# One step of a hybrid encoder: the sample's value tile in fp32 products side by side, w_o's adds on GpSimd, a key load and a memory key rearranged

## The chip, the cores and the metric

The kernel is one program on one core of a Trainium2 chip. The metric is device time in microseconds of that core: the median of three runs of the kernel before is 816.82 us (816.26 to 816.88). Engines are named as in the profile: PE (TensorE), DVE (VectorE), ACT (ScalarE), POOL (GpSimd) and SP (the queue that issues most DMAs).

## The reference, cut to what matters

One layer over 512 prompt and 64 sample tokens (576 in all, width 1024), in float32:

```python
h = rms_norm(x, g_mix)
z = h @ w_in                       # q_f, k_f, v_f, f_logit, c_q, c_kv, k_r
ckv = rms_norm(c_kv, g_ckv)        # returned, and expanded to keys and values
fox_o = attend(q_f, k_f, v_f, ...) # 8 heads x 64, forgetting gate, causal
mla_o = attend(mla_q, mk, mv, ...) # 8 heads, low-rank
mixed = concat([rms_norm(fox_o, g_fox_out), rms_norm(mla_o, g_mla_out)])
x = x + mixed @ w_o
m = rms_norm(mem, g_mem_src); mem_k, mem_v = m @ w_mk, m @ w_mv
x = x + attend(rms_norm(x, g_mem) @ w_mq, mem_k, mem_v) @ w_mo
hf = rms_norm(x, g_ffn)
x = x + (silu(hf @ w_gate) * (hf @ w_up)) @ w_down
return rms_norm(x, g_final), fox_k, fox_v, logf, ckv, kr, mem_k, mem_v
```

The change touches `v_f` (returned as fox_v) for the 64 sample tokens, the way of `ckv` to memory, the product with `w_o` for its fox half, and `mem_k`.

## The kernel before

**Numbers in two parts.** Nearly every weight product is made of three matmuls (`product`, L495 to L501): operand a is held as a high part in fp32r (`hhi`, `whi`) and a rest (`hlo`, `wlo`), and PE adds high x high, high x low and low x high. ACT makes the high parts (`split(b)`, the copy of L1121), POOL or DVE the rests (`rest(b)` at L2243, `weight_rest` at L1758). Some products are made in plain fp32 instead; each of those is two records of MATMUL in the trace (two passes over the moving operand), while a transposition and an fp32r product are one. `columns` (L517) sums squares over partitions with plain fp32 products by a column of ones; `spread` (L525) and `turn` (L658) are transpositions.

**Weights.** The layer's weights before the feed-forward part come in 49 blocks of the tensor `w_front`. SP's `load(b)` (L2410) brings block b into `wraw[:, b % 2]` as soon as the rest of block b-2 is made (`f_lo`), ACT's split fills `whi[:, b % 3]`, POOL's or DVE's rest `wlo[:, b % 3]`. So wraw is double and the parts are triple buffered. PE takes block b after `f_lo` has reached b+1.

**The value stage.** Blocks 7 to 10 are the value weights, 256 rows each (two k steps of 128). For each of the eight k, PE makes five token tiles: tokens stand still in the array (128, for the last tile 64), and 512 weight columns move. Sums lie in banks 0 to 4. After blocks 7, 8 and 9 come small fp32 groups (sums of squares, or spreads of their roots), which DVE and ACT turn into norms. DVE then scales the five tiles into `vst` (L1711), ACT copies them to `va`, SP sends them out. Next PE takes blocks 11, 12 and 13 (query and key weights) and goes over to attention.

**The key latents.** `ckvf` is scaled by DVE in two pieces (L1706, semaphore `s_kvn`). ACT makes `ckvhi` of each. SP sends the pieces out as `out_ckv` (L2455, `s_kvst`), and POOL, which makes the rests `ckvlo` (L2267), waits for `s_kvst` first. POOL's order is rest(11), ckvlo 0, rest(12), ckvlo 1, rest(13).

**Attention.** One loop over steps s from 0 to 95 is written out for each engine: at step s PE makes the scores of tile s (s below 80), a piece of other work (`filler`, at steps given by tables such as `WO_AT` and `RB_AT`), and the transposition of tile s-2. Other engines have the same loop and evict at step s what PE made at s-1. The filler at `WO_AT` is the product with the fox half of w_o, half a tile (128x288) each, 16 in all; DVE multiplies each by rstd into `evt` (L1847) and adds that to `xa` (L1849). The one at `RB_AT` spreads the reciprocal sums of a pair of heads; the last is at steps 86 and 87. PE leaves a spot in its banks 6 and 7 to be used again once DVE has evicted it (`spot_free`). The pieces `values(p)` (L676) and `sample_values(p)` (L692) multiply two heads at once: plain fp32, a stationary operand of 64 columns each, the results in the two halves of the partitions. `memory_keys(m)` makes a head of the memory's keys, eight k steps of three products.

Of the kernel before, what the change touches and what calls it, by code (L numbers as in the profile page):

```python
# [10 lines left out]
ALU = mybir.AluOpType  # L11
# [96 lines left out]
def build(nc, i_, o_, cum_dram):  # L108
# [93 lines left out]
    bias, _ = place("bias", [8, 3, NK], F32R, rbase + 2 * rsize)  # L202
    qt, _ = place("qt", [128, T], F32, sqbase)
# [43 lines left out]
    with ExitStack() as ctx:  # L247
# [78 lines left out]
        s_y, s_yst, d_half, s_xg = sem("s_y"), sem("s_yst"), sem("d_half"), sem("s_xg")  # L326
# [167 lines left out]
        def _(pe):  # L494
# [70 lines left out]
            columns(0, sqacc).then_inc(n_col, 1)  # L565
# [9 lines left out]

            pe.wait_ge(n_rs, 1)
# [4 lines left out]
            for c in range(4):  # L581
                b = B_V + c
                pe.wait_ge(f_lo, b + 1)
                for kk in range(2):
                    k = 2 * c + kk
                    for tt in range(TT):
                        a, n = 128 * tt, tok(tt)
                        mm = product(ps[0:n, tt, :], [t[:, k, a:a + n] for t in x1],
                                     [front(b, lo, 2, 512)[:, kk, :] for lo in (0, 1)], k == 0, k == 7)
                    if k == 0:  # L590
                        pe.wait_ge(s_cqacc, 2)
                        columns(5, sq2)
# [189 lines left out]
            def memory_keys(m):  # L782

                b = B_MK[m]
                pe.wait_ge(f_lo, b + 1)
                for k in range(KT):
                    mm = product(ps[:, m, 0:NM], [front(b, lo, KT, 128)[:, k, :] for lo in (0, 1)],
                                 [t[:, k, :] for t in (memh, meml)], k == 0, k == KT - 1)
                mm.then_inc(f_used[b % 3], 1)

            for s in range(LAST):
# [298 lines left out]
            for half in range(2):  # L1090
# [18 lines left out]
                if half == 0:  # L1109
                    mm.then_inc(d_half, 1)  # L1110
# [6 lines left out]
        def _(act):  # L1117
# [70 lines left out]
            act.wait_ge(s_init, 2)  # L1188
# [398 lines left out]
        def _(dve):  # L1587
# [31 lines left out]
            add_square(7)  # L1619
            dve.wait_ge(s_hlo, KT)  # L1620
            v.memset(vst[64:128, 6, :], 0.0).then_inc(s_init, 1)
# [87 lines left out]
            for tt in range(TT):  # L1709
                n = tok(tt)  # L1710
                v.tensor_scalar(vst[0:n, tt, :], ps[0:n, tt, :], small[0:n, S_RCM + tt:S_RCM + tt + 1], None, ALU.mult)\  # L1711
                    .then_inc(s_vev, 1)
# [76 lines left out]
            def evicted(s):  # L1789
# [431 lines left out]
            dve.wait_ge(d_half, 1)  # L2221
# [11 lines left out]
        def _(pool):  # L2233
# [69 lines left out]
            for s in range(LAST + 1):  # L2303
# [30 lines left out]
                if s - 1 in HIGH_AT and s not in (HIGH_AT[0] + 1, HIGH_AT[4] + 1):  # L2334
# [3 lines left out]
                    g.tensor_tensor(sqacc[:, 0:T], sqacc[:, 0:T], tmp2[:, j % 2, :], ALU.add).then_inc(s_oacc, 1)  # L2338

# [65 lines left out]
        def _(sp):  # L2405
            def load(b):

                need(sp, f_lo, b - 1)
                n = BLOCK_COLS[b]
# [24 lines left out]
            sp.wait_ge(s_init, 2)  # L2434
# [14 lines left out]
            load(12)  # L2449
            sp.dma_start(maskf[:, :], i_["consts"][:, C_MASK:C_MASK + 576]).then_inc(s_mask, 16)  # L2450
            sp.dma_start(maskm[:, :], i_["consts"][:, C_MASK + 576:C_END]).then_inc(s_mask, 16)
            sp.wait_ge(s_lf, 1)
            sp.dma_start(o_["logf"], lfk[:, 0:T]).then_inc(s_out, 16)
            sp.wait_ge(s_kvn, 2)
            sp.dma_start(o_["ckv"].rearrange("p (k n) -> p k n", k=2), ckvf[:, :, 0:T]).then_inc(s_kvst, 16)  # L2455
# [279 lines left out]
```

## Time and profile before

| | us |
|---|---|
| median of three runs | 816.82 |
| the profiled execution | 816.31 |
| its span in the trace | 814.4 |
| PE busy | 798.5 (98%) |
| DVE busy | 549.1 (67%) |
| ACT busy | 408.8 (50%) |
| POOL busy | 331.8 (41%) |

The profiled execution's time holds 1.9 us outside the span, and is 0.51 us under the median. Busy time of PE is the union of its instructions, which overlap: each record lasts some 0.15 us longer than the distance to the next start. So what an instruction costs on a full PE is the distance between starts, not its duration. The profile's granted clock of PE is at full speed (9 in tenths) in all but the last of the 40 slices.

### The profile page before, as it was taken

Reading aid. Unit: us, or ns where it says so; the run is one execution under the profiler, and the core shown is the slowest. Engines: PE = TensorE matmul, PEld = TensorE weight load, DVE = VectorE, ACT = ScalarE, POOL = GpSimd, SP = SyncE. Lnnn points to the kernel's source line nnn. Section 1 sums busy time; section 2 is a strip of 40 time slices with the busy share of each in tenths; the row PEclk is TensorE's granted clock in tenths of the full one; section 3 lists DMA queues with packets and bytes.
Section 4 is the critical chain, followed back from the end, with each engine's and each line's share of the span. In section 5 each row is a group of like instructions: output and inputs, shape, how many; then the busy total and the mean of one; then the engine's idle time right before and its main releaser. Section 6 shows DMA issues by size and latency. Waiting matters only on the chain.

```text
span 814.4 us, 15952 instructions
## 1 busy us (share of the span) xinstructions
PE 798.5 (98%) x5842; PEld 761.2 (93%) x5842; DVE 549.1 (67%) x986; ACT 408.8 (50%) x753; POOL 331.8 (41%) x242
## 2 busy tenths in 40 slices
PE   7999999999999999999999999999999999999996
PEld 7987998888988999998999999999999999999996
DVE  6355467887779748467599989998889985212213
ACT  7462475666777325555474555455554464322221
POOL 3664963383112126640654333333323336543420
PEclk9999999999999999999999999999999999999998
DMA  8333432110025234330133322223322332323103
GB/s 262 104 115 114 159 94 68 36 47 27 27 102 198 78 105 129 105 111 20 52 104 105 105 97 64 96 103 103 103 82 74 101 117 76 113 74 95 46 2 116
DMA packets 26518, 75.90 MB, mean 93 GB/s; under 512 B 2896, under 2 KB 7448, under 8 KB 26328
## 3 DMA queue, kind: packets, MB, share of 16 engines
q1 hardware_dynamic: 26176, 74.87, 28.7%
q8 instruction: 36, 0.59, 0.3%
q10 hardware_dynamic: 288, 0.30, 0.1%
q14 instruction: 18, 0.15, 0.1%
HBM read 68.62 MB, written 6.53 MB: 92 GB/s over the span
## 4 chain that ended last, share of the span: by engine, by line
PE 92%; DVE 3%; issue 2%; ACT 1%; DMA 0%; POOL 0%; DVEq 0%; ACTq 0%
PE ps L499 28%; PE ps L500 27%; PE ps L501 27%; PE ps L658 2%; PE ps L676 2%; PE ps L926 1%; PE ps L517 1%; PE ps L525 1%; DVE xb L2217 1%; PE ps L641 1%; PE ps L911 1%; PE ps L640 1%; DVE probs L1770 0%; ACT probs L1121 0%; DMA wraw<-w_front 0%
## 5 line engine op out<-in xcount | busy, mean ns | idle before, releaser
L499 PE MATMUL ps<-hhi,whi 128*128 128x288 f32 (+1 forms) x896 | 267.6, 299 | 6.1 <-DVE hlo L1609 5.7
L500 PE MATMUL ps<-hhi,wlo 128*128 128x288 f32 (+1 forms) x896 | 265.8, 297 | 0.0
L501 PE MATMUL ps<-hlo,whi 128*128 128x288 f32 x800 | 237.3, 297 | 0.0
L1121 ACT ACTIVATE whi<-wraw 128x1024 fp32r<-128x1024 f32 (+3 forms) x138 | 114.8, 838 | 135.6 <-PE ps L501 122.7
L499 PEld LDWEIGHTS ps<-hhi,whi 128*128 128x128 f32 x896 | 169.6, 189 | 7.7 <-DVE hlo L1609 5.7
L500 PEld LDWEIGHTS ps<-hhi,wlo 128*128 128x128 f32 x896 | 169.4, 189 | 0.2
L501 PEld LDWEIGHTS ps<-hlo,whi 128*128 128x128 f32 x800 | 151.1, 189 | 0.0
L2386 POOL TENSOR_TENSOR wlo<-wraw,whi 128x512 fp32r<-128x512 f32 x60 | 78.5, 1322 | 146.9 <-ACT whi L1121 146.9
L2243 POOL TENSOR_TENSOR wlo<-wraw,whi 128x256 fp32r<-128x256 f32 (+2 forms) x83 | 89.5, 1104 | 97.8 <-ACT whi L1121 97.6
L501 PE MATMUL ps<-hidlo,whi 128*128 128x288 f32 (+2 forms) x352 | 104.2, 296 | 0.0
L2400 POOL TENSOR_TENSOR wlo<-wraw,whi 128x1024 fp32r<-128x1024 f32 (+1 forms) x24 | 59.3, 2477 | 72.9 <-ACT whi L1121 72.9
L501 PE MATMUL ps<-tl,whi 128*128 128x288 f32 x240 | 71.5, 298 | 0.0
L500 PE MATMUL ps<-th,wlo 128*128 128x288 f32 x240 | 71.4, 298 | 0.0
L499 PE MATMUL ps<-th,whi 128*128 128x288 f32 x240 | 71.0, 296 | 0.0
L1121 ACT ACTIVATE whi<-ss 128x512 fp32r<-128x512 f32 x61 | 38.3, 631 | 63.7 <-PE ps L501 36.5
L501 PEld LDWEIGHTS ps<-hidlo,whi 128*128 128x128 f32 x352 | 66.3, 188 | 0.0
L2188 DVE TENSOR_TENSOR tmp<-ps,rstd 128x576 f32<-128x576 f32 (+2 forms) x9 | 6.2, 690 | 87.1 <-PE ps L501 87.1
L500 PE MATMUL ps<-hidhi,wlo 128*128 128x288 f32 (+2 forms) x192 | 57.0, 297 | 0.0
L499 PE MATMUL ps<-hidhi,whi 128*128 128x288 f32 (+2 forms) x192 | 57.0, 297 | 0.0
L1121 ACT ACTIVATE probs<-probs,small 128x128 f32<-128x128 f32 (+4 forms) x72 | 40.1, 557 | 32.8 <-DVE small L1770 32.4
L499 PEld LDWEIGHTS ps<-th,whi 128*128 128x128 f32 x240 | 45.3, 189 | 0.0
L500 PEld LDWEIGHTS ps<-th,wlo 128*128 128x128 f32 x240 | 45.2, 188 | 0.0
(292 smaller groups left out, 1799.4 us busy)
## 6 DMA issues: line engine op xcount, KB each, us to landing
wraw<-w_ff SPq DMA_DIRECT2D x44, 512.0 KB, 4.1
wraw<-w_front SPq DMA_DIRECT2D x41, 512.0 KB, 3.7
wraw<-w_down SPq DMA_DIRECT2D x16, 512.0 KB, 3.6
wraw<-w_down SPq DMA_DIRECT2D x8, 384.0 KB, 3.2
wraw<-w_front SPq DMA_DIRECT2D x7, 384.0 KB, 3.6
xa<-x_t SPq DMA_DIRECT2D x8, 288.0 KB, 4.8
xs<-x_t SPq DMA_DIRECT2D x7, 288.0 KB, 5.6
out_fox_k<-kt SPq DMA_DIRECT2D x4, 288.0 KB, 2.5
```

Source lines behind the costliest of these rows:

```text
L499: nc.tensor.matmul(out, lh, rh, start=start, stop=False)
L500: nc.tensor.matmul(out, ll, rh, start=False, stop=False)
L501: return nc.tensor.matmul(out, lh, rl, start=False, stop=stop)
L517: mm = nc.tensor.matmul(ps[:, bank, at + tt:at + tt + 1], source[:, 128 * tt:128 * tt + 128], ones[:, 0:1], start=True, stop=True)
L525: mm = nc.tensor.transpose(out[:, at:at + n], col[0:n, tt:tt + 1].to_broadcast([n, 128]), ident[0:n, 0:n])
L640: nc.tensor.matmul(out, q1[r][:, q], k1[r][:, ks], start=True, stop=False)
L658: mm = nc.tensor.transpose(ps[:, 2 + s % 2, 128 * kb:128 * kb + 128], probs[:, P_AT[u] + 128 * kb:P_AT[u] + 128 * kb + 128], ident[:, :])
L676: mm = nc.tensor.matmul(ps[64 * e:64 * e + 64, 4, 128 * kb:512], va[:, g, kb, h + e, :], pt[e][:, 512 * kb:512 * kb + 512 - 128 * kb], sta ...
L1121: return nc.scalar.activation(out, src, func, **kw)
L2243: mm = g.tensor_tensor(wlo[:, b % 3, c], wraw[:, b % 2, c], f(whi[:, b % 3, c]), ALU.subtract)
L2386: g.tensor_tensor(w_operand(1, j), src, f(w_operand(0, j)), ALU.subtract).then_inc(g_lo, 1)
L2400: g.tensor_tensor(ffw(n, 1, 1, w)[:, 0, :], (wraw2, wraw)[n % 4 // 2][:, n % 2, 0:w], f(ffw(n, 0, 1, w)[:, 0, :]), ALU.subtract).then_inc( ...
```

## The change

Four edits, and some semaphores that follow from them.

1. **The sample's value tile.** DVE makes one new tile `hs`, the 64 sample tokens times the gain in plain fp32, and PE multiplies it with the unsplit weights in `wraw`: per k step two products, columns 0 to 255 into partitions 0 to 63 of bank 4 and columns 256 to 511 into partitions 64 to 127, each with 64 stationary and 256 moving columns. The three products of 64 x 512 per k step go. The new products stand at the head of each of the four blocks (`sample_part`). Since PE now reads `wraw`, the loads of blocks 9 to 12 wait for it too (`p_part`), and the mask loads are issued ahead of block 12's. The fifth column of the first sums of squares is made twice, for both halves of the partitions, and DVE scales the tile in two pieces of 64x256.
2. **w_o's adds.** The 16 adds of `evt` to `xa` go from DVE to POOL, a step's turn after DVE's multiply. DVE waits for the add before last before it writes the same half of `evt` again.
3. **The key latents' way out** is issued from ACT's queue, between its two copies, and no longer from SP's.
4. **Memory key 0** is made in two parts: k steps 0 to 5 at step 85, where all eight were, and 6 and 7 at step 87, behind the last RB transpositions.

```diff
@@ build
+    hs, c2 = place("hs", [128, KT, TS], F32, rbase + rsize - 2 * NK * 4)
@@ tensor
-            columns(0, sqacc).then_inc(n_col, 1)
+            columns(0, sqacc, 4)
+            for e in range(2):
+                mm = nc.tensor.matmul(ps[64 * e:64 * e + 64, 0, 4:5], sqacc[:, TP:T], ones[:, 0:1], start=True, stop=True)
+            mm.then_inc(n_col, 1)
...
+            def sample_part(b):
+
+                for k in (2 * (b - B_V), 2 * (b - B_V) + 1):
+                    for e in range(2):
+                        at = 512 * (k % 2) + 256 * e
+                        mm = nc.tensor.matmul(ps[64 * e:64 * e + 64, 4, 0:256], hs[:, k, :], wraw[:, b % 2, at:at + 256],
+                                              start=k == 0, stop=k == 7)
+                mm.then_inc(p_part, 1)
+
+            pe.wait_ge(s_init, 2)
...
                 pe.wait_ge(f_lo, b + 1)
+                sample_part(b)
                 for kk in range(2):
                     k = 2 * c + kk
-                    for tt in range(TT):
-                        a, n = 128 * tt, tok(tt)
-                        mm = product(ps[0:n, tt, :], [t[:, k, a:a + n] for t in x1],
+                    for tt in range(4):
+                        a = 128 * tt
+                        mm = product(ps[:, tt, :], [t[:, k, a:a + 128] for t in x1],
...
                 if s == 85:
-                    memory_keys(0)
+                    memory_keys(0, 0, 6)
                 elif s == 87:
+                    memory_keys(0, 6, KT)
@@ scalar
-            for j in range(2):
-                act.wait_ge(s_kvn, j + 1)
-                activation(ckvhi[:, j, :], ckvf[:, j, :]).then_inc(s_kvhi, 1)
+            act.wait_ge(s_kvn, 1)
+            activation(ckvhi[:, 0, :], ckvf[:, 0, :]).then_inc(s_kvhi, 1)
+            act.wait_ge(s_kvn, 2)
+            nc.scalar.dma_start(o_["ckv"].rearrange("p (k n) -> p k n", k=2), ckvf[:, :, 0:T]).then_inc(s_kvst, 16)
+            activation(ckvhi[:, 1, :], ckvf[:, 1, :]).then_inc(s_kvhi, 1)
@@ vector
+            v.tensor_tensor(hs[:, :, :], xs[:, :, TP:T], gains[:, G_MIX:G_MIX + KT].unsqueeze(2).to_broadcast([128, KT, TS]), ALU.mult)\
+                .then_inc(s_init, 1)
...
-                        if s == at:
-                            dve.wait_ge(s_x[m], 32)
-                            if m == 0:
-                                dve.wait_ge(s_fev, nth(FR_AT + 1) + 1)
+                        if s == at and m == 0:
+                            dve.wait_ge(s_fev, nth(FR_AT + 1) + 1)
+                        need(dve, s_xa1, 2 * m + half - 1)
                         v.tensor_tensor(evt[:, c], spot(n, HT), rstd[:, c], ALU.mult).then_inc(s_fev, 1)
-                        dve.wait_ge(s_fev, n + 1)
-                        v.tensor_tensor(xa[:, m, c], xa[:, m, c], evt[:, c], ALU.add).then_inc(s_xa1, 1)
@@ gpsimd
+                for m, at in enumerate(WO_AT):
+                    if s - 1 in (at, at + 1):
+                        half = s - 1 - at
+                        c = slice(half * HT, half * HT + HT)
+                        if half == 0:
+                            pool.wait_ge(s_x[m], 32)
+                        pool.wait_ge(s_fev, nth(s - 1) + 1)
+                        g.tensor_tensor(xa[:, m, c], xa[:, m, c], evt[:, c], ALU.add).then_inc(s_xa1, 1)
@@ sync
                 need(sp, f_lo, b - 1)
+                if B_V + 2 <= b < B_V + 6:
+                    sp.wait_ge(p_part, b - B_V - 1)
...
```

What this makes of the order of instructions is shown at three places. The first is PE between the value stage's first and second block. `sqacc` is the sum of squares of the latents, `hhi` and `hlo` the tokens, `whi` and `wlo` the weights; a row names the moving operand's and the stationary operand's tiles. Before:

```order
L501 MATMUL ps<-wlo,hhi 128x512
L499 MATMUL ps<-whi,hhi 64x512
L500 MATMUL ps<-whi,hlo 64x512
L501 MATMUL ps<-wlo,hhi 64x512
L517 MATMUL ps<-ones,sqacc 128x1 [waits s_kvacc]
L517 MATMUL ps<-ones,sqacc 128x1 x4
L499 MATMUL ps<-whi,hhi 128x512 [waits f_lo]
L500 MATMUL ps<-whi,hlo 128x512
```

and after the change:

```order
L503 MATMUL ps<-wlo,hhi 128x512
L519 MATMUL ps<-ones,sqacc 128x1 [waits s_kvacc]
L519 MATMUL ps<-ones,sqacc 128x1 x4
L586 MATMUL ps<-wraw,hs 64x256 [waits f_lo]
L586 MATMUL ps<-wraw,hs 64x256 x3
L501 MATMUL ps<-whi,hhi 128x512
L502 MATMUL ps<-whi,hlo 128x512
```

The three products with 64 tokens that end each k step are gone, and four plain fp32 products with `hs` stand once per block, behind the small fp32 group.

The second place is DVE at steps 78 to 80 of the attention loop, where `pt` is the copy of transposed scores that PE's next transposition and values wait for. Before:

```order
L1847 TENSOR_TENSOR evt<-ps,rstd 128x288 [waits s_fdone]
L1849 TENSOR_TENSOR xa<-xa,evt 128x288 [waits s_fev]
L1888 SCALAR_TENSOR_TENSOR hlo<-olof,gains,hhi 128x576 [waits s_osq,s_ohi]
L1773 TENSOR_REDUCE small<-ps 64x1 [waits s_ex,s_qk]
L1847 TENSOR_TENSOR evt<-ps,rstd 128x288 [waits x_tile1,s_fdone]
L1849 TENSOR_TENSOR xa<-xa,evt 128x288 [waits s_fev]
L1783 COPY pt_73<-ps 128x3x128 [waits s_pvp,s_tr]
L1847 TENSOR_TENSOR evt<-ps,rstd 128x288 [waits s_fdone]
L1849 TENSOR_TENSOR xa<-xa,evt 128x288 [waits s_fev]
L1877 RECIPROCAL small<-small 128x10 [waits s_rb,s_ex]
```

and after:

```order
L1871 TENSOR_TENSOR evt<-ps,rstd 128x288 [waits s_fdone]
L1910 SCALAR_TENSOR_TENSOR hlo<-olof,gains,hhi 128x576 [waits s_osq,s_ohi]
L1798 TENSOR_REDUCE small<-ps 64x1 [waits s_ex,s_qk]
L1871 TENSOR_TENSOR evt<-ps,rstd 128x288 [waits s_xa1,s_fdone]
L1808 COPY pt_73<-ps 128x3x128 [waits s_pvp,s_tr]
L1871 TENSOR_TENSOR evt<-ps,rstd 128x288 [waits s_xa1,s_fdone]
L1899 RECIPROCAL small<-small 128x10 [waits s_rb,s_ex]
```

The adds to `xa` are gone from between the copy of `pt` and what stood ahead of it; the multiplies into `evt` now wait for POOL's adds (`s_xa1`).

The third place is SP's queue from the output of the rotary key on. Before, with blocks 11 and 12 in one row (x2) and `out_ckv` in the queue:

```order
L2447 DMA out_kr<-krf 32x576 [waits s_kr]
L2410 DMA wraw<-w_front 128x1024 [waits f_lo] x2
L2450 DMA maskf<-consts 128x576
L2451 DMA maskm<-consts 128x512
L2453 DMA out_logf<-lfk 8x576 [waits s_lf]
L2455 DMA out_ckv<-ckvf 256x1x576 [waits s_kvn]
L2410 DMA wraw<-w_front 128x1024 [waits f_lo]
```

and after:

```order
L2479 DMA out_kr<-krf 32x576 [waits s_kr]
L2442 DMA wraw<-w_front 128x1024 [waits p_part,f_lo]
L2481 DMA maskf<-consts 128x576
L2482 DMA maskm<-consts 128x512
L2442 DMA wraw<-w_front 128x1024 [waits p_part,f_lo]
L2485 DMA out_logf<-lfk 8x576 [waits s_lf]
L2442 DMA wraw<-w_front 128x1024 [waits f_lo]
```

Block 12's load has moved behind the two mask loads and waits for PE (`p_part`), and `out_ckv` is no longer in this queue.

## Rows read from the trace of the kernel before

**Rows 1.** The page: span, and part 1 (engine, busy us, share, instructions).

```profile
span 814.4 us, 15952 instructions
PE 798.5 (98%) x5842; PEld 761.2 (93%) x5842; DVE 549.1 (67%) x986; ACT 408.8 (50%) x753; POOL 331.8 (41%) x242
```

**Rows 2.** Busy time by stretch: the value stage (us and count of each engine).

```profile
47.87:79.74 31.87, 31.87 (x152) 24.60 (x151) 13.98 (x19) 14.40 (x17) 16.01 (x17) 1.00 0.41 128
```

**Rows 3.** Timeline of PE, value stage: start us, us, engine line op out<-in xcount.

```profile
50.68 0.39 PE L499 MATMUL ps<-whi,hhi 128*64 128x512 f32 x1
...
51.37 1.17 PE L517 MATMUL ps<-ones,sq 128*128 128x1 f32 x10
52.40 0.48 PE L499 MATMUL ps<-whi,hhi 128*128 128x512 f32 x1
52.72 0.40 PE L500 MATMUL ps<-whi,hlo 128*128 128x512 f32 x1
```

**Rows 4.** Timeline of PE: first pair of heads, two 64-column halves side by side.

```profile
123.44 2.37 PE L676 MATMUL ps<-pt,va 128*64 128x512 f32 x16
125.74 0.40 PE L499 MATMUL ps<-hhi,whi 128*128 128x288 f32 x1
...
128.11 0.57 PE L692 MATMUL ps<-pt,va 128*64 128x64 f32 x12
128.61 0.44 PE L658 MATMUL ps<-ident,probs 128*128 128x128 f32 x2
```

**Rows 5.** Timeline of PE: the sample's values of the last pair of heads.

```profile
265.00 0.29 PE L501 MATMUL ps<-hlo,whi 128*128 128x288 f32 x1
265.22 0.57 PE L692 MATMUL ps<-pt,va 128*64 128x64 f32 x12
265.72 0.40 PE L499 MATMUL ps<-hhi,whi 128*128 128x288 f32 x1
```

**Rows 6.** Timeline of PE, steps 81 and 82 (L658 is the transposition of step 79).

```profile
259.84 0.27 PE L761 MATMUL ps<-ident,rb 128*128 128x128 f32 x1
260.62 0.52 PE L658 MATMUL ps<-ident,probs 128*128 128x128 f32 x3 [0.51 <-DVE pt L1783]
261.12 0.65 PE L676 MATMUL ps<-pt,va 128*64 128x512 f32 x2
```

**Rows 7.** Timeline of DVE just before that.

```profile
256.68 1.34 DVE L1849 TENSOR_TENSOR xa<-xa,evt 128x288 f32<-128x288 f32 x1
...
259.54 0.46 DVE L1849 TENSOR_TENSOR xa<-xa,evt 128x288 f32<-128x288 f32 x1
259.92 0.55 DVE L1783 COPY pt<-ps 128x384 f32<-128x384 f32 x1
```

**Rows 8.** Timeline of POOL at the same place.

```profile
256.28 1.42 POOL L2338 TENSOR_TENSOR sqacc<-sqacc,tmp 128x576 f32<-128x576 f32 x1 [6.11 <-ACT tmp L1121]
```

**Rows 9.** Timeline of PE after memory key 0, and two products of key 1.

```profile
274.11 0.51 PE L517 MATMUL ps<-ones,msq 128*128 128x1 f32 x4
274.94 0.40 PE L499 MATMUL ps<-hhi,whi 128*128 128x288 f32 x1 [0.33 <-DVE olof L1832]
...
281.66 0.28 PE L499 MATMUL ps<-memh,whi 128*128 128x256 f32 x1
281.78 0.28 PE L500 MATMUL ps<-memh,wlo 128*128 128x256 f32 x1
```

**Rows 10.** Timeline of SP's queue: block 12's load, the latents' way out.

```profile
63.30 0.33 SPq L2410 DMA_DIRECT2D wraw<-w_front  x1
...
74.32 0.65 SPq L2455 DMA_DIRECT2D out_ckv<-ckvf  x1
```

**Rows 11.** Timeline of POOL: low parts of the latents and of block 12.

```profile
78.20 1.98 POOL L2267 TENSOR_TENSOR ckvlo<-ckvf,ckvhi 128x832 fp32r<-128x832 f32 x1 [7.96 <-DMA out_ckv<-ckvf]
80.14 2.84 POOL L2243 TENSOR_TENSOR wlo<-wraw,whi 128x256 fp32r<-128x256 f32 x4
```

**Rows 12.** Timeline of PE: the first product with block 12.

```profile
86.14 0.30 PE L499 MATMUL ps<-hhi,whi 128*128 128x288 f32 x1
```

More of the change, by code:

```diff
@@ L202, in build @@
     bias, _ = place("bias", [8, 3, NK], F32R, rbase + 2 * rsize)
+    hs, c2 = place("hs", [128, KT, TS], F32, rbase + rsize - 2 * NK * 4)
+    assert c2 <= rbase + rsize - NK * 4
     qt, _ = place("qt", [128, T], F32, sqbase)
@@ L325, in build @@
         w_vec, w_copy, t_f, x_hf, s_dsc = sem("w_vec"), sem("w_copy"), sem("t_f"), sem("x_hf"), sem("s_dsc")
-        s_y, s_yst, d_half, s_xg = sem("s_y"), sem("s_yst"), sem("d_half"), sem("s_xg")
+        s_y, s_yst, p_part, s_xg = sem("s_y"), sem("s_yst"), sem("p_part"), sem("s_xg")
         past = slice(T, NK)
@@ L780, in filler, with memory_keys @@
                 mm.then_inc(s_fdone, 1)
-            def memory_keys(m):
+            def memory_keys(m, k0=0, k1=KT):
                 b = B_MK[m]
                 pe.wait_ge(f_lo, b + 1)
-                for k in range(KT):
+                for k in range(k0, k1):
                     mm = product(ps[:, m, 0:NM], [front(b, lo, KT, 128)[:, k, :] for lo in (0, 1)],
                                  [t[:, k, :] for t in (memh, meml)], k == 0, k == KT - 1)
-                mm.then_inc(f_used[b % 3], 1)
+                if k1 == KT:
+                    mm.then_inc(f_used[b % 3], 1)
             for s in range(LAST):
@@ L1109, in _ @@
                 if half == 0:
-                    mm.then_inc(d_half, 1)
+                    mm.then_inc(p_part, 1)
             pe.wait_ge(r_sq, 16 + KT + 1)
@@ L1187, in _ @@
             act.wait_ge(s_cv, 48)
-            act.wait_ge(s_init, 2)
+            act.wait_ge(s_init, 3)
             for t in (5, 6):
@@ L1619, in _ @@
             add_square(7)
+            v.tensor_tensor(hs[:, :, :], xs[:, :, TP:T], gains[:, G_MIX:G_MIX + KT].unsqueeze(2).to_broadcast([128, KT, TS]), ALU.mult)\
+                .then_inc(s_init, 1)
             dve.wait_ge(s_hlo, KT)
+            dve.wait_ge(s_init, 2)
             v.memset(vst[64:128, 6, :], 0.0).then_inc(s_init, 1)
@@ L1708, in _ @@
             used(dve, B_V + 3)
[L1709 to L1712, printed above, removed]
+            for tt in range(4):
+                v.tensor_scalar(vst[:, tt, :], ps[:, tt, :], small[:, S_RCM + tt:S_RCM + tt + 1], None, ALU.mult).then_inc(s_vev, 1)
+            for e in range(2):
+                a = slice(64 * e, 64 * e + 64)
+                mm = v.tensor_scalar(vst[0:64, 4, 256 * e:256 * e + 256], ps[a, 4, 0:256], small[a, S_RCM + 4:S_RCM + 5], None, ALU.mult)
+            mm.then_inc(s_vev, 1)
             def query_dup(c):
@@ L2220, in _ @@
             low, high = slice(0, LAST_AT[1]), slice(LAST_AT[1], T)
-            dve.wait_ge(d_half, 1)
+            dve.wait_ge(p_part, 5)
             residual(KT - 1, KT - 1, low, ps[:, 6, 0:low.stop], lambda a: a)
@@ L2433, in _ @@
                 load(b)
-            sp.wait_ge(s_init, 2)
+            sp.wait_ge(s_init, 3)
             sp.wait_ge(s_sq, KT)
@@ L2448, in _ @@
             load(11)
-            load(12)
             sp.dma_start(maskf[:, :], i_["consts"][:, C_MASK:C_MASK + 576]).then_inc(s_mask, 16)
             sp.dma_start(maskm[:, :], i_["consts"][:, C_MASK + 576:C_END]).then_inc(s_mask, 16)
+            load(12)
             sp.wait_ge(s_lf, 1)
             sp.dma_start(o_["logf"], lfk[:, 0:T]).then_inc(s_out, 16)
-            sp.wait_ge(s_kvn, 2)
-            sp.dma_start(o_["ckv"].rearrange("p (k n) -> p k n", k=2), ckvf[:, :, 0:T]).then_inc(s_kvst, 16)
             load(13)
```

## The prediction, on record before the changed kernel ran

> **What bounds the kernel now.** I read the page first: PE is busy 798.5 us of a span of 814.4 [rows 1]. A full PE can still be waiting inside that number, since records overlap, so I went on to the stretch that the largest edit touches: in the value stage, 47.87 to 79.74, PE is busy all 31.87 us at a clock of 1.00 [rows 2]. There and nearly everywhere the distance between the starts of two matmuls is what counts: work taken off PE comes off the time, work added adds to it, and the other engines matter only where PE waits for them. The timeline has few such waits; two lie at places that the change touches: before the transposition at 260.62 and before the product at 274.94 [rows 6, 9].
>
> **Part 1, the value tile: what goes.** One k step's three products of 64 tokens by 512 columns run from 50.68 to 51.37 [rows 3]: 0.695 us (0.69 in the rows' rounding), 0.232 each, no less than with 128 tokens. There are eight k steps: 8 x 0.695 = 5.56 us go.
>
> **What comes.** 16 plain fp32 products, 64 stationary and 256 moving columns, in pairs for the two halves of the partitions. The trace has this form: `values` multiplies two heads side by side. Its 16 records (4 pairs of 512, 384, 256 and 128 columns, 2 passes each) take 123.44 to 125.74 = 2.30 us, which I count as 2 x 1280 = 2560 columns of pairs; `sample_values` has 6 passes of 64 = 384 columns in 128.11 to 128.61 = 0.50 us [rows 4]. The difference, 1.80 us for 2176 columns, is 0.212 us per pass of a pair of 256. Whether the two members truly run together, or in turn at a pace like fp32r's (5120 columns at 0.232 per 512 would be 2.32 us), these rows can't tell; the new products have the same form, so the price is the same. The new work is 8 pairs x 2 passes x 0.212 = 3.39 us.
>
> A visit to the half-width form costs something by itself. From [rows 4]: 0.50 - 1.5 x 0.212 = 0.18 us between first start and the next instruction's. Before it, 265.00 to 265.22 is 0.22 where 288 columns take 0.13 (256 take 0.12 [rows 9]): 0.09 more [rows 5]. Behind it, the first fp32r product takes about 0.1 longer, as behind the sums of squares (52.40 to 52.72 is 0.32 against 0.23 [rows 3]). So a visit from fp32r and back is 0.18 + 0.09 + 0.10 = 0.37. Block 7 pays that. Blocks 8 to 10 are entered from a small fp32 group whose way back is paid already: I take 0.27 for the one behind the sums of squares, and 0.18 for the two behind spreads, which end in another array form. Sum 1.00 us.
>
> What the row shows first: 0.09 us in and 0.18 around each visit. The Trainium skill (TensorEngine Tiling, Tiling Modes, Key Properties) says that changing the tiling mode, as opposed to the tile, drains TensorE. Our trace agrees. A reader who counted only the columns would have -2.17 us for this part; with the drains it is little over half of that.
>
> The first sums of squares: five full columns take 1.03 us [rows 3], 0.21 each. Now four, and two of half width: about 0.40 (0.18 + 0.09 + 2 x 0.053, and a little for the way out) for 0.21, +0.19 us.
>
> Part 1 on PE: -5.56 + 3.39 + 1.00 + 0.19 = **-0.98 us**. Bounds: -2.0 if all entries but one are free, -0.4 if every visit costs 0.37 and more.
>
> DVE's new multiply for `hs` falls into the first half of the start-up phase, ahead of a memset; the memset and SP's loads of old values wait for it, some 0.6 us, long before use. Evicting the tile in two pieces adds some 0.2 us on DVE, beside 12 us of products with blocks 11 and 12. I take nothing for either; without cover they'd cost what they last.
>
> **The held loads.** Four loads now wait for PE's new products, and block 12's moves from 63.30 [rows 10] to after the head of the fourth block, some 47.87 + 3 x 7.8 + 1.1 = about 72.5. ACT's split and the other chains on ACT slip by 2 to 3 us at block 9. Block 12 is the tightest: POOL does ckvlo 0 first, which waits for `out_ckv`, issued at 74.32 and landed at 78.20 [rows 10, 11], 3.9 us. Moved to ACT's queue it starts about 0.5 us earlier in absolute time, and so do its inputs; but block 12, block 13 and the latents are now under way together. With a landing at 78.5: ckvlo 0 till 80.5, block 12's rest (2.84 us [rows 11]) till 83.4. PE wants it at 86.14 - 1.0 = 85.1 [rows 12]. Slack 1.7 us, so nothing.
>
> **Part 2, the adds.** The wait before the transposition at 260.62: start to start 0.78 from 259.84, where such a transposition takes 0.11, and the group itself 0.50 to 261.12 for some 0.35: 0.67 + 0.15 = 0.82 us [rows 6]. The row names DVE's copy of `pt`, which began at 259.92, the moment the add from 259.54 was through [rows 7]; ahead of it DVE was late already through the add at 256.68, which took 1.34 us. Without the adds the copy starts at least 0.38 us earlier, probably over 0.6. But the values at 261.12 also wait for ACT's copy of the tile before, which hangs on the same DVE chain through an exponential, and follows it only in part. I take **-0.45 us**, bounds 0 and -0.82. What would be late next is that copy of ACT's. POOL is mostly idle there; an add is half of its 576-wide one, 1.42 / 2 = 0.7 us [rows 8], and the final multiply-add of xa comes microseconds later.
>
> **Part 3, key 0 in two parts.** The product at 274.94 waited for DVE to evict the spread of a pair of heads: 0.83 us for the four records from 274.11, where ten take 1.03 [rows 3, 9], so 0.42 of stall. Six products of 256 columns (6 x 0.12 = 0.7 us) now stand inside it and cover it wholly; they had to be made anyway. Their own change from transposition to fp32r and back costs some 0.15. **-0.27 us**, bounds +0.15 and -0.42. Block 27 comes free 0.5 us later for ACT's split of 30, whose user is 5 us off.
>
> **Sum.** -0.98 - 0.45 - 0.27 = -1.70 us. Profiled execution: 816.31 - 1.70 = 814.61, which is 0.51 under the median shown; against the median of 816.82 that is **815.1 us**. Own range of this case 814.2 to 816.0. All later stages are PE's in the same way, so what is won by 300 stays won.
>
> **Rivals.**
> *The port.* [rows 7, 8]: DVE's add of 256.68, two operands in SBUF, lasted 1.34 us where the others last 0.46, and ended 0.3 us after POOL's 256.28 + 1.42 = 257.70: it stood behind POOL's instruction. By this kernel's trace, then, 16 new POOL adds of 0.7 us can each hold a DVE instruction of that kind (`hlo`, `meml`, `wlo`), which costs more than the 0.46 that DVE saves: 3 adds before the hand-off x 0.25 = 0.75 later rather than earlier. Sum: -0.98 - 0.27 + 0.75 = -0.5, 816.3. Against it: the DVE instruction right behind the multiply starts before the semaphore reaches POOL, and then POOL stands behind it. The skill (GPSIMD Engine Reference, Specifications) states the sharing for just such instructions, those with two SBUF inputs; the trace agrees. Chance 0.17.
> *The late block*, slower than before. If the three transfers land together late, 6 us after issue, near 80, and POOL's rest takes 4 us instead of 2.84 because DVE is at work, block 12 is ready at 80 + 2 + 4 = 86 and more, and block 14's load, which waits for it in SP's queue, holds back the rests of the first keys: PE waits at 85 and again at the first scores. It decides from a landing of 80.3 us on; with 3.5 us of waits in all the sum is +1.8, 818.6; with 1.5 us it is no change. For it: queueing of a kind that no transfer there had before. Chance 0.08.
> *Not side by side.* In `values` each half has its own operands. If two halves with the same stationary tile and one block of moving weights take twice as long, that is 3.39 more: +1.7, 818.5. Against it: in [rows 4] too the form is all that the array sees. Chance 0.03.
> *More.* Both waits gone and entries cheap: -2.0 - 0.8 - 0.4 = -3.2, 813.6. Chance 0.05.
> The forecast has the rest, 0.67.
>
> **How the numbers follow.** 0.2% is 1.6 us, about what can be told from no change, and my sum sits at that line. Of the forecast's 0.67 I count 0.44 as faster and 0.23 as same; "more" is faster; the port is same but for 0.02; the late block is half slower, half same; the third is slower. Faster 0.51, same 0.42, slower 0.07. Range 813.6 to 817.0: the port's 816.3 and the mild late block are in it, the strong ones out.
>
> **What would show it.** L586 (the new products): 32 records at starts 0.21 apart in pairs, four groups, 0.3 to 0.4 us of extra at each; the value stage 1.1 to 1.2 us shorter (the columns' 0.19 lie ahead of it). No idle time of PE between 80 and 99. The transposition near 259 waits under 0.3 us. No wait at the product behind `msq`'s columns. DVE's two-input instructions in 254 to 262: if several last over 1 us, the port rival is at work. I am wrong if the value stage is not shorter by at least 0.5 us, or if PE idles before its first product with block 12, 13 or the first scores.

## The result and the profile after

| | median us | runs |
|---|---|---|
| before | 816.77 (815.94 to 817.55) | 17 |
| changed | 818.3 (816.83 to 818.89) | 17 |

The ratio is 1.0016, with a 95% interval of 1.0009 to 1.0022: the changed kernel is slower by 0.7 to 1.8 us. Forecast were 815.1, and 817.0 as the upper end. The profiled execution of the changed kernel took 816.83, the lowest of its 17; by how much and why is told below.

The page of the changed kernel (span and part 1, as in [rows 1]):

```profile
span 814.8 us, 15994 instructions
PE 797.5 (98%) x5852; PEld 759.7 (93%) x5852; DVE 544.3 (67%) x972; ACT 409.0 (50%) x753; POOL 346.8 (43%) x258
```

PE has 1.0 us less to do and the span is 0.4 longer: work was taken away and waits came in. Busy time by stretch finds them. The first row is the value stage, which answers to [rows 2]; the second goes from its end to the first scores (us, then busy us and count of PE, PEld, DVE, ACT, POOL, then granted clock, DMA share, GB/s):

```profile
47.74:78.30 30.56, 30.56 (x159) 23.47 (x159) 12.12 (x19) 14.74 (x17) 11.99 (x16) 1.00 0.40 121
78.30:100.10 21.80, 19.64 (x145) 19.22 (x144) 10.72 (x13) 10.35 (x13) 18.12 (x18) 1.00 0.44 149
```

The value stage is full, and 1.3 us shorter than 31.87. The next stretch has the same 145 records as before, but PE is idle for 2.16 us of it. Before, the same stretch lasted 19.20 us and was full. PE's timeline of the changed kernel at the two places:

```profile
84.61 0.30 PE L503 MATMUL ps<-hlo,whi 128*128 128x288 f32 x1
86.46 0.37 PE L501 MATMUL ps<-hhi,whi 128*128 128x288 f32 x1 [1.55 <-POOL wlo L2265]
...
99.19 0.29 PE L503 MATMUL ps<-hlo,whi 128*128 128x288 f32 x1
100.10 0.30 PE L656 MATMUL ps<-k,q 128*128 128x128 f32 x1 [0.62 <-issue]
```

86.46 is the first product with block 12 [rows 12]. From the start before it 1.85 us pass where 0.13 are normal: 1.7 us lost. 100.10 is the first product of scores; 0.91 after the start before it, so another 0.8 lost. "issue" hides a wait for several semaphores; GpSimd's timeline names it. Here is POOL, and ahead of it ACT's queue and SP's queue of the same kernel:

```profile
73.26 0.67 ACTq L1220 DMA_DIRECT2D out_ckv<-ckvf  x1
```

```profile
65.30 0.33 SPq L2442 DMA_DIRECT2D wraw<-w_front  x1
...
72.75 0.33 SPq L2442 DMA_DIRECT2D wraw<-w_front  x1
73.12 0.33 SPq L2485 DMA_DIRECT2D out_logf<-lfk  x1
73.50 0.33 SPq L2442 DMA_DIRECT2D wraw<-w_front  x1
```

```profile
81.59 1.98 POOL L2289 TENSOR_TENSOR ckvlo<-ckvf,ckvhi 128x832 fp32r<-128x832 f32 x1 [8.59 <-DMA out_ckv<-ckvf]
83.53 2.78 POOL L2265 TENSOR_TENSOR wlo<-wraw,whi 128x256 fp32r<-128x256 f32 x4
86.27 2.19 POOL L2289 TENSOR_TENSOR ckvlo<-ckvf,ckvhi 128x832 fp32r<-128x832 f32 x1
88.42 3.05 POOL L2265 TENSOR_TENSOR wlo<-wraw,whi 128x256 fp32r<-128x256 f32 x4
91.55 2.92 POOL L2298 TENSOR_TENSOR q<-qt,q 64x576 fp32r<-64x576 f32 x2
94.55 3.42 POOL L2265 TENSOR_TENSOR wlo<-wraw,whi 128x256 fp32r<-128x256 f32 x4
98.04 4.01 POOL L2309 TENSOR_TENSOR k<-kt,k 64x832 fp32r<-64x832 f32 x2
```

The output of the latents goes out at 73.26, between the loads of block 12 (72.75) and block 13 (73.50), and lands 8.2 us later; before it took 3.7 (issue at 74.32 [rows 10]; ckvlo 0, which waits for the landing, starts at 78.20 [rows 11]). POOL stands still for 8.59 us in front of ckvlo 0 (7.96 before) and then works without a gap to 102: block 12's rest is ready at 86.31 and frees PE at 86.46, and the low parts of the first keys come out last of all and free the scores at 100.10. So one late landing is paid for twice.

The DMA traffic by queue shows what happened in those 8.2 us. Two stretches of the changed kernel, 73.5 to 77.3 and 77.3 to 81.5 (queue, kind: packets, MB, share of the 16 engines; q1 is SP's, q10 ACT's):

```profile
q1 hardware_dynamic: 262, 0.96, 94.7%
q10 hardware_dynamic: 2, 0.00, 0.3%
```

```profile
q10 hardware_dynamic: 270, 0.59, 36.0%
q1 hardware_dynamic: 58, 0.19, 13.0%
```

For almost 4 us the engines carry the two loads and hardly anything else, although the output was issued ahead of block 13's; 270 of its 272 packets move after 77.3.

**How shifts are counted.** The start-up varies from one execution to the next, whatever the change: the first column sums (33.15 in the profile before) began 0.30 us earlier in the changed kernel's profile and 0.1 to 2.0 us later in those of the experiments. Below, "shift" is the start of a record against the same record before, less the shift at those column sums. The profile before was itself an early one, the changed kernel's the earliest of all. That is part of why its 816.83 lies below its median of 818.3; how early the other executions started up isn't known.

Shifts of the changed kernel: -1.14 at the last value product (the stage's 1.3 less the 0.17 that the column sums and the way in add ahead of it), +1.46 at the first scores, +1.68 at a transposition near 219, +0.99 at the last transposition near 261, +0.91 at the last of the memory keys near 301, +0.95 at the last column sums near 807.

### The profile page after: what moved, and what is told of

Same layout as the page of the kernel before. It is cut to its first block, busy times and chain, and to the rows that moved or that the text cites. A ratio compares the mean times of both kernels' runs of the same rounds, so it can differ in the third digit from the quotient of the medians.

```text
span 814.8 us, 15994 instructions
## 1 busy us (share of the span) xinstructions
PE 797.5 (98%) x5852; PEld 759.7 (93%) x5852; DVE 544.3 (67%) x972; ACT 409.0 (50%) x753; POOL 346.8 (43%) x258
## 4 chain that ended last, share of the span: by engine, by line
PE 91%; DVE 3%; issue 2%; ACT 2%; DMA 1%; POOL 1%; DVEq 0%; ACTq 0%; POOLq 0%
PE ps L501 28%; PE ps L502 27%; PE ps L503 27%; PE ps L674 2%; PE ps L692 2%; DMA out_ckv<-ckvf 1%; PE ps L944 1%; PE ps L519 1%; POOL wlo L2265 1%; PE ps L527 1%; DVE xb L2239 1%; PE ps L657 1%; PE ps L929 1%; PE ps L656 1%; DVE probs L1795 0%
## 5 line engine op out<-in xcount | busy, mean ns | idle before, releaser
L2416 POOL TENSOR_TENSOR wlo<-wraw,whi 128x512 fp32r<-128x512 f32 x60 | 78.5, 1323 | 146.9 <-ACT whi L1139 146.9
```

The source lines that it names most:

```text
L2416: g.tensor_tensor(w_operand(1, j), src, f(w_operand(0, j)), ALU.subtract).then_inc(g_lo, 1)
```

## The experiments

Each was timed in 5 rounds against the kernel before (medians 816.77 to 817.0 in the three groups of four). Shifts are of the profiled execution. The 95% intervals of the ratio are some 0.0018 wide (1.5 us), so parts of 0.3 us are told by the trace, not by the medians. A landing is that of one profiled execution, and it scatters: the value tile alone (5.5 us) and the output on SP ahead of load 13 (6.4) have the same transfers at the same times up to there (loads at 66.4, 73.9 and 75.3, the output at 74.6), and so have, but for the start-up, block 10's passes early (5.1) and both cures (6.4). So landings less than some 1.3 us apart aren't told from each other.

| kernel | out_ckv: issue to landing | shift, last value product | first scores | end | median | ratio |
|---|---|---|---|---|---|---|
| before | 3.7 | 0 | 0 | 0 | 816.77 | 1 |
| changed | 8.2 | -1.14 | +1.46 | +0.95 | 818.3 | 1.0016 |
| changed, again | 7.8 | -1.14 | +1.08 | +0.63 | 817.9 | 1.0013 |
| output on SP, behind load 13 | 7.0 | -1.14 | +0.88 | +0.33 | 817.06 | 0.9999 |
| output on SP, ahead of load 13 | 6.4 | -1.13 | -0.05 | -0.64 | 815.66 | 0.9984 |
| value tile alone | 5.5 | -1.13 | -0.79 | -0.49 | 816.52 | 0.9998 |
| block 10's passes early | 5.1 | -1.31 | -0.75 | -1.17 | 815.63 | 0.9988 |
| load 13 held | 4.8 | -1.14 | -0.99 | -1.78 | 814.91 | 0.9977 |
| latents' output alone | 3.3 | 0 | 0 | 0 | 816.85 | 0.9998 |
| ckvlo later | 8.2 | -1.14 | -0.99 | -1.81 | 815.03 | 0.9979 |
| both cures | 6.4 | -1.30 | -1.32 | -2.15 | 814.92 | 0.9973 |
| adds alone | 3.7 | 0 | 0 | -0.29 | 816.21 | 0.9994 |
| key 0 alone | 3.7 | 0 | 0 | -0.53 | 816.56 | 0.9995 |
| before, ckvlo later | 3.7 | 0 | 0 | 0 | 816.85 | 0.9998 |

### Is it the queue or the held load? The output back on SP

```diff
-            nc.scalar.dma_start(o_["ckv"].rearrange("p (k n) -> p k n", k=2), ckvf[:, :, 0:T]).then_inc(s_kvst, 16)
...
+            sp.wait_ge(s_kvn, 2)
+            sp.dma_start(o_["ckv"].rearrange("p (k n) -> p k n", k=2), ckvf[:, :, 0:T]).then_inc(s_kvst, 16)
             load(13)
```

> The changed kernel with the key latents' output issued again by SP, after the wait for the normed latents and before block 13's load; everything else as changed. Theory (held load): the output lands late because block 12's load, which now waits for the value tile's products, is in flight with it, whatever queue issues the output. Then the output still lands at 79.5 to 82, GpSimd's first low part of the latents starts then, the first product with block 12 stays at 86.0 to 86.8 and the time is within 0.7 us of the changed kernel's (817.6 to 819). Rival (the queue): on ScalarE's queue the transfer is served badly beside SP's; put back on SP's it lands by 78, the first product with block 12 comes by 85.2, and the time is 815.5 to 816.5.

815.66, ratio 0.9984 (0.9975 to 0.9993). The theory of the held load alone failed here, since its time was to be 817.6 or more: the landing did fall, from 8.2 to 6.4 us, and of 2.60 us between the last value product and the first scores 1.08 stayed (0.2 at block 12, 0.7 at the scores). Its time is inside the rival's range. But the rival, that ScalarE's queue is served badly, isn't shown by it: on SP the output had also passed ahead of block 13's load. The packets say so. Between 76.9 and 78.2, ahead of the first packet of block 13's load at 78.19, this kernel's engines moved:

```profile
q1 hardware_dynamic: 194, 0.43, 97.2%
```

That is 2.2 KB a packet: rows of the output (2304 bytes), not of a load (4096 bytes).

### The other order on the same queue

```diff
+            load(13)
             sp.wait_ge(s_kvn, 2)
             sp.dma_start(o_["ckv"].rearrange("p (k n) -> p k n", k=2), ckvf[:, :, 0:T]).then_inc(s_kvst, 16)
-            load(13)
```

> The changed kernel with the latents' output on SP's queue again, but behind block 13's load instead of ahead of it. Theory A (three transfers share the engines and the last served lands 8 to 9 us after the first issue): the output lands 81.0 to 82.5 as it did on ScalarE's queue, the two waits are as in the changed kernel and the time is within 0.6 of it. Theory B (ScalarE's queue is served worse than its bytes account for): it lands before 80.5 and the time is at most 816.8.

817.06, ratio 0.9999 (0.9990 to 1.0008). SP's queue, then POOL of this kernel:

```profile
73.37 0.33 SPq L2441 DMA_DIRECT2D wraw<-w_front  x1
73.74 0.33 SPq L2484 DMA_DIRECT2D out_logf<-lfk  x1
74.11 0.33 SPq L2441 DMA_DIRECT2D wraw<-w_front  x1
74.49 0.65 SPq L2487 DMA_DIRECT2D out_ckv<-ckvf  x1
```

```profile
81.61 1.98 POOL L2288 TENSOR_TENSOR ckvlo<-ckvf,ckvhi 128x832 fp32r<-128x832 f32 x1 [8.12 <-DMA out_ckv<-ckvf]
```

By the trace it is nearly theory A: with both loads ahead of it the output lands at 81.5 on SP's queue too, and PE loses 1.1 us at block 12 and 0.8 at the scores. Issued on ACT's queue ahead of block 13's load, it was served as if it stood behind it. So most of what the queue cost is the place that it gave. The time is outside what theory A allowed (within 0.6): 1.2 us under the changed kernel's first median, 0.8 under the second; the end shift is +0.33 against +0.63 to +0.95. Theory B asked for 816.8 at most and a landing before 80.5, and has neither. With the start-up taken off, ckvlo 0 starts 0.2 to 0.6 us earlier than in the two profiles of the changed kernel, which is less than the scatter of a landing; whether ACT's queue costs that little by itself stays open.

### The latents' output alone on the kernel before

The edit is the third part of the change, and the masks' loads ahead of block 12's.

> The kernel before with one part of the change alone: the latents' output on ScalarE's queue between the two casts, and the masks' loads ahead of block 12's. Block 12's load is not held by the value products here (it goes out at 64 to 65). Theory (held load): the output has only block 13's load beside it and lands at 76.5 to 78.5, first scores as before at 98.9 within 0.3, the time 816.8 within 0.4 of the kernel before. Rival (the queue): the output lands after 80 here as well, block 12's rest is late, first scores 0.8 or more later, the time 817.6 to 818.6.

816.85, ratio 0.9998 (0.9989 to 1.0007): the theory. On ACT's queue, with block 12's load long through (issued at 63.95) and block 13's at 71.02, the output lands in 3.3 us, less than before. Nothing moves on PE.

### Block 13's load held till the output has landed

```diff
             sp.dma_start(o_["logf"], lfk[:, 0:T]).then_inc(s_out, 16)
+            sp.wait_ge(s_kvst, 16)
             load(13)
```

> The changed kernel with one more wait on SP: block 13's load goes out only when the latents' output has landed. Theory A (both loads beside it): with block 12's load alone beside it the output lands at 77.5 to 79 instead of 81.46, the first product with block 12 comes by 85.2, and, as block 13 is read only at 87 and later, the time is 816.0 to 817.2. Theory B (block 12's load alone makes it late): it lands after 80 as before, block 13's load goes out after 80, and the time is 818 or more. Rival (queue): likewise after 80, since the output stays on ScalarE's queue.

814.91, ratio 0.9977 (0.9967 to 0.9986). Theory A, and 1.1 us under the range that it gave. SP's queue, then POOL:

```profile
73.57 0.33 SPq L2442 DMA_DIRECT2D wraw<-w_front  x1
73.94 0.33 SPq L2485 DMA_DIRECT2D out_logf<-lfk  x1
78.87 0.33 SPq L2442 DMA_DIRECT2D wraw<-w_front  x1
```

```profile
78.99 1.98 POOL L2289 TENSOR_TENSOR ckvlo<-ckvf,ckvhi 128x832 fp32r<-128x832 f32 x1 [5.35 <-DMA out_ckv<-ckvf]
```

With one load beside it the output needs 4.8 us. A load that goes out 5 us later makes the kernel faster by 3.4 us against the changed one's first median, by 3.0 against its second: block 13 was never urgent.

### Block 10's passes one block early

```diff
-                sample_part(b)
+                if c < 3:
+                    sample_part(b)
+                if c == 2:
+                    pe.wait_ge(f_load[(b + 1) % 2], 16 * ((b + 1) // 2 + 1))
+                    sample_part(b + 1)
```

> The changed kernel with the value tile's four last passes (block 10's) made one block earlier, behind those of block 9, so that block 12's load isn't held to 72.7 but goes out at 66 to 68, well ahead of the latents' output, which stays on ScalarE's queue. Theory (held load): the output has block 13's load alone beside it and lands 3.3 to 5.5 us after its issue; the first product with block 12 comes without a wait, first scores 2 us earlier than in the changed kernel, time 814.9 (814.4 to 815.5). Rival (the queue alone): the landing still takes over 7 us, the time is over 816.5. Beside that a visit to the narrow tile is saved, about 0.2.

815.63, ratio 0.9988 (0.9979 to 0.9997). Block 12's load went out at 69.03 (66.7 by the start-up of the changed kernel's profile) and the output landed in 5.1 us. No wait for block 12; at the first scores 0.57 us stayed, and the time is 0.1 us over the range expected. The visit saved is there: the shift at the last value product is -1.31 instead of -1.14.

### The waiter moved away from the landing

```diff
-            rest(11)
-            for j in range(2):
-                pool.wait_ge(s_kvhi, j + 1)
-                pool.wait_ge(s_kvst, 16)
-                g.tensor_tensor(ckvlo[:, j, :], ckvf[:, j, :], f(ckvhi[:, j, :]), ALU.subtract).then_inc(s_kvlo, 1)
-                rest(12 + j)
+            for b in range(11, 14):
+                rest(b)
```

The removed three lines for each j stand again behind POOL's first build of `rb`, at step 12 of attention's loop.

> The changed kernel with GpSimd's two low parts of the latents moved from ahead of the rests of blocks 12 and 13 to the first gap in attention (at 125 us; TensorE first reads them at 157), so that nothing that TensorE wants soon waits for the output's landing. All theories expect the output to land as late as in the changed kernel. Theory (late block): the first product with block 12 comes at 84.8 within 0.4 (86.46 in the changed kernel), first scores at 97.5 to 98.5 (100.10), the time 815.7 (815.0 to 816.4). Rival (the loss lies elsewhere, in GpSimd's adds beside VectorE or in the later stages): the stage is shorter by 2 us but the time stays over 817.2.

815.03, ratio 0.9979 (0.9970 to 0.9988): the theory. The output is as late as ever (8.2 us), and nobody minds. POOL of this kernel, then PE at the first scores:

```profile
78.27 5.62 POOL L2265 TENSOR_TENSOR wlo<-wraw,whi 128x256 fp32r<-128x256 f32 x8 [4.67 <-ACT whi L1139]
87.28 2.92 POOL L2294 TENSOR_TENSOR q<-qt,q 64x576 fp32r<-64x576 f32 x2 [3.39 <-ACT q L1139]
```

```profile
98.23 0.30 PE L503 MATMUL ps<-hlo,whi 128*128 128x288 f32 x1
98.37 0.22 PE L656 MATMUL ps<-k,q 128*128 128x128 f32 x1
```

Both waits are gone. This is the cleanest proof: neither the transfers nor PE's work were touched, only what stands in POOL's order behind a landing, and 3.3 us came back against the changed kernel's first median, 2.9 against its second. From the traces it is 2.45 us at the first scores and 2.76 at the end; 0.22 of the loss had been added inside attention.

> The kernel before with GpSimd's two low parts of the latents in attention's gap at 125 us, and nothing of the change. Theory (the landing costs only where it decides): TensorE has no wait for block 12 or at the first scores in the kernel before, so the time stays, 816.8 within 0.3. Rival (the fix is a gain of its own, which would then be wrongly counted as the cure of the change): 816.3 or less, with attention shorter.

The same move on the kernel before: 816.85, ratio 0.9998 (0.9989 to 1.0007), no shift. POOL's wait cost nothing there, so the gain above is the cure of the change and not a gain of its own.

### The parts alone, and the changed kernel again

> The kernel before with the value tile's part of the change alone (gains-scaled sample columns, products side by side, the loads of blocks 9 to 12 held for them, the masks' loads ahead of block 12's); the latents' output stays on SP behind block 12's load. Theory (late block): the stage up to the last value product is 1.2 us shorter, but the output still lands only 6 to 7 us after its issue (about 80), the first product with block 12 waits 0.1 to 0.5 and the first scores 0.5 to 0.9 for GpSimd, so 0.3 to 0.7 is left: 816.2 (815.9 to 816.5) beside 816.85 before. Forecast's own step without a late block: 815.8 or less. Rival (the tile's edit costs elsewhere): 816.9 or more.

816.52, ratio 0.9998 (0.9989 to 1.0007). The output landed in 5.5 us, where 6 to 7 were expected, and PE has no wait at block 12. In the trace the shift at the last value product is -1.13, and 0.35 is lost by the first scores (0.19 of it a wait there), 0.3 more till the end: -0.49. Part 1 drags the late output in even without part 3, since it holds block 12's load.

> The kernel before with GpSimd making the eight adds of w_o's scaled pieces alone. Theory: the transposition's wait of 0.67 near 260 shrinks to under 0.3 and the value products behind it wait 0.3 to 0.4 for ScalarE: net gain 0.4, time 816.4 (816.1 to 816.7), attention ahead of 240 unchanged within 0.1. Rival (the port): GpSimd's adds hold up VectorE's work and the time is 816.9 or more, with TensorE waits for VectorE that the kernel before does not have.

816.21, ratio 0.9994 (0.9985 to 1.0003); by the trace -0.29 (it is sixteen adds, not eight). PE at the place of [rows 6]:

```profile
259.97 0.27 PE L761 MATMUL ps<-ident,rb 128*128 128x128 f32 x1
260.08 0.49 PE L658 MATMUL ps<-ident,probs 128*128 128x128 f32 x3
260.83 1.08 PE L676 MATMUL ps<-pt,va 128*64 128x512 f32 x4 [0.25 <-ACT pt L1121]
```

The transposition starts 0.11 after the record before it, where it took 0.78: all of the wait of 0.67 is gone. The values behind it start 0.75 after it, where it was 0.50: against the 0.35 that the group takes, they are 0.40 late, waiting for ACT, where it was 0.15.

> The kernel before with the first memory key's product in two parts alone (six of its eight contraction tiles at step 85, two at step 87). Theory: the stage from 256 to 275 is 0.35 shorter (0.25 to 0.5) since the wait of 0.47 behind the column sums goes, time 816.5 (816.2 to 816.8). Rival (the wait only moves, to the second part's end or the row after it): 816.8 within 0.2.

816.56, ratio 0.9995 (0.9986 to 1.0004); by the trace -0.45 behind the key and -0.53 at the end. PE behind the second part of key 0, at the place of [rows 9]:

```profile
275.19 0.28 PE L501 MATMUL ps<-meml,whi 128*128 128x256 f32 x1
275.31 0.50 PE L517 MATMUL ps<-ones,msq 128*128 128x1 f32 x4
275.67 0.38 PE L499 MATMUL ps<-hhi,whi 128*128 128x288 f32 x1
```

From the column sums to the next product it is 0.36 us, where [rows 9] have 0.83.

> The changed kernel itself once more, beside the same runs of the kernel before as the three others of this group. By its earlier runs 818.1 within 0.5; its output lands 7.5 to 8.5 us after its issue, both waits (first product with block 12: 1.2 to 2, first scores: 0.5 to 1) are there, and from the first column sums on it loses 0.7 to 1.2 us on the kernel before.

817.9, ratio 1.0013 (1.0004 to 1.0022); landing 7.8 us, 1.3 lost at block 12, 0.8 at the scores. The two waits are as expected, and the end shift of +0.63 is just under the 0.7 to 1.2 expected; this profile has a start-up like most.

### A version that beats both

Block 10's passes early and POOL's two low parts late, together.

> Both cures on the changed kernel: block 10's passes of the value tile behind block 9's, and GpSimd's low parts of the latents in attention's gap. By the stages measured: value stage 1.31 shorter than before (one visit saved), no wait till the last key transposition, adds and key parts 0.82, together 2.0 under the kernel before: 814.8 (814.3 to 815.3), 0.1 to 0.3 under the run with the later low parts alone. If both waits were not the whole loss it stays over 815.5.

814.92, ratio 0.9973 (0.9963 to 0.9983): 2.1 us under the kernel before in its group and, across groups, 3.4 under the changed one. It can't be told from the runs with the load held or with the low parts alone moved, whose intervals overlap with its own.

## Why the prediction was wrong, step by step

- **What bounds the kernel: right.** PE's starts carried every term, and the other engines mattered only where PE waited.
- **Part 1 on PE, forecast -0.98: right, somewhat low.** Measured -1.13 or -1.14 in all seven profiles that have the edit as it stands. PE's timeline of the changed kernel:

```profile
47.52 0.29 PE L503 MATMUL ps<-hlo,whi 128*128 128x288 f32 x1
47.74 1.08 PE L586 MATMUL ps<-wraw,hs 128*64 128x256 f32 x8
48.76 0.50 PE L501 MATMUL ps<-whi,hhi 128*128 128x512 f32 x1
49.09 0.40 PE L502 MATMUL ps<-whi,hlo 128*128 128x512 f32 x1
```

From 47.52 to 49.09 it is 1.57 us. Less 0.13 and 0.23 for the two fp32r products that stand there anyway and 4 x 0.212 for the passes, 0.36 remain; 0.37 was forecast for such a visit, from groups that were of another use [rows 3 to 5]. The passes of a pair stand 0.215 apart, so *Not side by side* fell. The part off was the first column sums: +0.07 in place of +0.19.
- **"The held loads ... slack 1.7 us, so nothing": the step that failed.** It set the landing at 78.5, 4.7 us after an issue at 73.8: only 0.8 more than the 3.9 read where nothing stood ahead, though two loads were now to go out beside it. It took 8.2 us, landed at 81.46, and cost 1.7 + 0.8 us on PE, with 0.22 more in attention. The numbers for a better step were there: 576 KB took 3.7 us with nothing ahead, and two loads of 512 KB were to go out within a microsecond of it. Taken one behind another at that pace, the 1600 KB are some 10 us from the first issue, by my estimate; the trace shows 8.7 (72.75 to 81.46). What was missing was to add up the bytes under way. The text named this as *the late block*, with the right chain (block 12, then block 14's load and the first keys) and a point of decision, a landing of 80.3; the experiments order themselves by that. With each run's start-up shift taken off, ckvlo 0 starts at 78.5 (load 13 held), 79.5 (value tile alone), 79.6 (block 10's passes early), 80.3 (output ahead of load 13), 81.3 (behind it), 81.5 and 81.9 (the changed kernel twice), and from the last value product to the first scores 0.15, 0.34, 0.56, 1.08, 2.02, 2.22 and 2.60 us are lost: about a microsecond for each one of delay, from some 79.3 on rather than 80.3. (Of these, 0.15 isn't the landing's: with the low parts moved away it is lost too.) For the product with block 12 the forecast's 80.3 was right: it waits 0.2 us there and not at all at 79.6. It is the first scores that wait from 79.3 on. The forecast also said that it would be wrong if PE idled before its first product with block 12 or the first scores, and PE did both. Its chance of 0.08 was the mistake.
- **Part 2, forecast -0.45: sign and mechanism right, size -0.29.** What was named as late next, ACT's copy, is what PE waits for. *The port* was in part at work: of the changed kernel, DVE and POOL, each at the same moment:

```profile
257.69 2.02 DVE L1910 SCALAR_TENSOR_TENSOR hlo<-olof,gains,hhi 128x576 fp32r<-128x576 f32 x1
```

```profile
257.67 1.43 POOL L2360 TENSOR_TENSOR sqacc<-sqacc,tmp 128x576 f32<-128x576 f32 x1 [0.63 <-ACT tmp L1139]
259.04 1.33 POOL L2368 TENSOR_TENSOR xa<-xa,evt 128x288 f32<-128x288 f32 x1
```

  The DVE instruction lasts 0.81 in the kernel before. It stretched by 1.2 us beside POOL's, though the first of POOL's two was there before the change as well; before, DVE's own add was stretched so instead ([rows 7], 1.34). GpSimd's own adds took 0.80 to 1.72 us (median 0.87), not 0.7. The rival's +0.75 did not come. The Trainium skill (GPSIMD Engine Reference, Specifications), cited ahead, says that the two engines share their interfaces to SBUF, with contention when VectorE's instruction has two SBUF inputs; these rows agree, and no run here separates the part that the new adds have in it.
- **Part 3, forecast -0.27: right in sign, too low, and past the bound of -0.42.** It was -0.45 to -0.53. The whole distance of 0.47 between [rows 9] and the rows of key 0 alone went; the charge of 0.15 for changing the form of product and back isn't seen.
- **The sum.** -1.14 - 0.29 - 0.53 = -1.96, and with the late landing cured the traces show -1.8 and, with a visit less, -2.15. With it the traces say +0.6 to +0.95 and the medians +0.9 to +1.5. The two parts of the change that made the landing late did no work at all: one held a load, the other moved the output to ACT's queue. Neither costs that much alone. The value tile with its held load, the output still on SP, ends at -0.49 instead of -1.13, 0.6 us; the output on ACT's queue, no load held, costs nothing; and putting the output back on SP in the changed kernel gives back 1.6 of the 2.8 us (+0.95 to -0.64). It is the two together that put the output behind both loads.

Still open: why block 13's load, issued on SP's queue 0.24 us after the output on ACT's, was served ahead of it. The size of the packets alone (2304 bytes against 4096) doesn't put the output last, since on SP's queue it passed ahead of that load with the same packets; whether it plays a part between two queues no run shows.

## What to carry to other kernels

When an edit makes a load wait, write down what else will be under way at its new time, and add up the bytes: in all runs here the output's packets moved only when those of the loads issued ahead of it were through or nearly so, and from ACT's queue in the changed kernel also those of a load issued just behind it. Then look at who stands behind that landing in an engine's order; the cheapest cure was not to speed up the transfer but to move the waiting instruction, whose result wasn't wanted for another 70 us, behind the work that was wanted at once (in the kernel before, holding up nothing, the same move brought nothing). And price each part by the shift that it leaves several stages later: here three parts kept their gains of 1.1, 0.3 and 0.5 us, and one late landing took all of it back.

## What the runs showed that was not expected

- A transfer issued on ACT's queue 0.24 us before a load on SP's moved 2 of its 272 packets in the 3.8 us in which that load and the one before it moved. From ACT's queue the output landed after 3.3 us with the load before it ahead by 4 us, after 4.8 with one load out 0.5 us before, and after 8.2 with a second one 0.2 us behind.
- The same transfers issued at the same times landed up to 1.3 us apart in two profiled executions (5.1 and 6.4, 5.5 and 6.4).
- A visit from fp32r products of 128 rows to fp32 products of 64 cost 0.36 us beside its columns, as the groups of another use had shown; two visits made one saved 0.17 us (a shift of -1.31 against -1.14 at the last value product).
- The start-up differs by up to 2.3 us between profiled executions at the first column sums, with the same code there or nearly so. A difference of under 1 us between two profiles is read from a common record behind the start-up, not from their spans.
